# Branch products of a token mixer's merge as three fp32r products of split operands, with part of a later gate's work moved

## What is computed

```python
mod = silu(c) @ ada_w + ada_b            # 1024 -> 6 * 1024
shift1, scale1, gate1, shift2, scale2, gate2 = split(mod, 6)
...
ya = einsum('bsw,wd->bsd', o_att, w_branch_att)     # 512 -> 1024
yh = einsum('bsw,wd->bsd', o_hg, w_branch_hg)       # 512 -> 1024
g = sigmoid(gate_logits)                            # two gates of 1024
merged = g[:, :, 0] * ya + g[:, :, 1] * yh
x = x + gate1 * (merged @ w_out)
h = rms_norm(x, norm_ffn_w) * (1 + scale2) + shift2
x = x + gate2 * expert_choice_ffn(h, ...)
```

## Time and profile before

| what | us |
|---|---|
| runs of before, lowest / median / highest | 2107.93 / 2107.97 / 2111.01 |
| the profiled execution's own time | 2108.66 |
| its span | 2106.9 |
| branch products, first record | 393.07 |
| output product, first record | 499.2 |
| output product, last addition by DVE | 548.3 |
| first expert matmul | 594.75 |

### The profile page before, as it was taken

The page is one execution under the profiler, slowest core; times in us unless marked ns, Lnnn a source line. Parts: engine busy times, 40 slices in busy tenths (PEclk is TensorE's granted clock), DMA queues, the critical chain, the costliest instruction groups (busy, mean ns, idle before and its releaser), DMA issues.

```text
span 2106.9 us, 20424 instructions
## 1 busy us (share of the span) xinstructions
PE 1923.8 (91%) x8738; PEld 1153.0 (55%) x8738; DVE 670.3 (32%) x931; ACT 448.6 (21%) x673; POOL 28.7 (1%) x41
## 2 busy tenths in 40 slices
PE   5999989999689999898988998888899999999998
PEld 5876766567444343343434334342344588888887
DVE  5474474475411110202011010201129623222333
ACT  5357446212211000010100001010020313222222
POOL 0000000000000000000000000000030000000000
PEclk9999999999889999999999999999999999999999
DMA  7311210584669999999999999999951032332311
GB/s 296 97 44 41 63 38 21 202 283 174 259 253 416 417 418 418 417 416 417 416 416 417 418 418 417 417 416 416 380 163 60 20 100 85 96 100 100 100 60 40
DMA packets 149183, 513.42 MB, mean 244 GB/s; under 512 B 8035, under 2 KB 74723, under 8 KB 114147
## 3 DMA queue, kind: packets, MB, share of 16 engines
q1 hardware_dynamic: 144720, 487.95, 59.3%
q10 hardware_dynamic: 4374, 24.18, 3.0%
HBM read 510.00 MB, written 2.10 MB: 243 GB/s over the span
## 4 chain that ended last, share of the span: by engine, by line
PE 67%; DMA 21%; DVE 6%; ACT 4%; issue 2%; SPq 0%; POOL 0%; ACTq 0%; DVEq 0%; POOLq 0%
DMA work<-in_w_exp_up 13%; PE ps L1100 11%; PE ps L1061 6%; DMA ring<-in_w_exp_up 6%; PE ps L1263 5%; PE ps L521 5%; PE ps L1222 4%; PE ps L1223 4%; PE ps L1224 4%; PE ps L537 3%; PE ps L539 3%; PE ps L538 3%; PE ps L988 3%; PE ps L544 3%; PE ps L720 2%
## 5 line engine op out<-in xcount | busy, mean ns | idle before, releaser
L1061 PE MATMUL ps<-work 128*64 128x512 f32 x1208 | 331.4, 595 | 34.9 <-DMA work<-in_w_exp_up 34.9
L1061 PE MATMUL ps<-ring,work 128*64 128x512 f32 x720 | 218.8, 595 | 19.8 <-DMA ring<-in_w_exp_up 19.8
L1061 PEld LDWEIGHTS ps<-work 128*64 128x64 f32 x1208 | 112.0, 137 | 209.5 <-issue 142.3
L2167 DVE TENSOR_TENSOR work<-work,ps 64x512 f32<-64x512 f32 x64 | 42.0, 692 | 495.2 <-ACT work L1629 494.5
L1629 ACT ACTIVATE work<-ps 64x512 f32<-64x512 f32 x64 | 32.6, 584 | 751.1 <-PE ps L1061 751.1
L521 PE MATMUL ps<-work,ring 128*128 128x512 f32 x320 | 138.9, 592 | 0.7 <-issue 0.7
L1100 PE MATMUL ps<-work 128*64 128x512 f32 x568 | 135.4, 630 | 4.2 <-issue 3.6
L1061 PEld LDWEIGHTS ps<-ring,work 128*64 128x64 f32 x720 | 71.7, 137 | 122.8 <-issue 84.4
L1222 PE MATMUL ps<-xh,wh 128*128 128x512 f32 x352 | 137.0, 389 | 0.0
L1224 PE MATMUL ps<-xh,wl 128*128 128x512 f32 x352 | 136.9, 389 | 0.0
L1223 PE MATMUL ps<-xl,wh 128*128 128x512 f32 x352 | 136.9, 389 | 0.0
(11 more groups left out here) (311 smaller groups left out, 2531.7 us busy)
## 6 DMA issues: line engine op xcount, KB each, us to landing
work<-in_w_exp_gate SPq DMA_DIRECT2D x76, 1024.0 KB, 24.5
work<-in_w_exp_up SPq DMA_DIRECT2D x75, 1024.0 KB, 25.9
work<-in_w_exp_down SPq DMA_DIRECT2D x71, 1024.0 KB, 21.0
ring<-in_w_exp_gate SPq DMA_DIRECT2D x45, 1024.0 KB, 24.5
ring<-in_w_exp_up SPq DMA_DIRECT2D x45, 1024.0 KB, 25.5
ring<-in_w_exp_down SPq DMA_DIRECT2D x42, 1024.0 KB, 22.0
ring<-in_w_in SPq DMA_DIRECT2D x27, 1024.0 KB, 6.4
work<-in_ada_w ACTq DMA_DIRECT2D x16, 1024.0 KB, 6.1
```

The lines of the kernel that those rows point to most:

```text
L1061: i = e.matmul(PS[64 * gu:64 * gu + 64, fb, :], at(XET + 128 * k + 64 * z, 64), flat(key)[:, 512 * fb:512 * fb + 512], start=(k == 0), sto ...
```

## The change

The branch products go from `dense_T` to a new function `branch` with three fp32r products. Their operands are split in new places: the pieces `cb` by `cb_hi` (ACT) and `cb_lo` (DVE), the two branches' outputs by copies `OAH`, `OHH` (ACT) and subtractions `OAL`, `OHL` (DVE). For d = 0 the recurrence product comes first. The first gate's row and the second shift's columns go from d = 6 behind units 0 and 1 of the output product, and their evacuations with them. The first piece of `w_out` is loaded behind the last `cb` piece, into another slot; `x` is loaded in two halves, the first two chunks later. The cycle of the experts' slots and the conditions of their first use are adapted.

```diff
-    i = more.index(("c0", 3))
+    i = len(more)
-    slots.insert(len(slots) - len(more) + i, 16)
+    slots.insert(len(slots) - len(more) + i, 14)
-    cycle = (12, 13, 14, 15, 8, 16, 2, 4, 7, 11, 9, 10, 1, 5, 3, 0, 6)
+    cycle = (2, 13, 12, 16, 15, 8, 7, 11, 14, 4, 9, 10, 1, 5, 3, 0, 6)
...
                 if key == ("wo", 0):
-                    e.wait_ge(s["mg_m"], 1)
+                    e.wait_ge(s["mg_pb"], 6)
...
-                    if slot in (8, 2):
+                    if slot in (2, 13):
                         e.wait_ge(s["wo_pe"], 4)
+                    elif slot == 8:
+                        e.wait_ge(s["ac_pe"], 4)
+                        e.wait_ge(s["ar_pe"], 2)
                     elif slot in (9, 10, 1, 3):
                         e.wait_ge(s["wo_pe"], 8)
-                    elif slot in (12, 13, 14):
+                    elif slot in (12, 16):
                         e.wait_ge(s["mg_pb"], 8)
-                        e.wait_ge(s["mg_m"], 4)
```

On PE:

```diff
+            def branch(bk, half, j, off, hi, lo, each=None):
+                wl = FWL[plan["cb", half][0]]
+                for k in range(4):
...
+                    e.matmul(bank(bk), CBH[half][:, w], hi[:, x], start=(k == 0), stop=False)
+                    e.matmul(bank(bk), CBH[half][:, w], lo[:, x], start=False, stop=False)
+                    p = e.matmul(bank(bk), wl[:, w], hi[:, x], start=False, stop=(k == 3))
+                return p
...
                 if j == 0:
-                    e.wait_ge(*got[kb])
-                if d == 6:
-                    e.wait_ge(s["d_ada"], 16)
-                    e.wait_ge(s["mg_a"], 6)
-                    ada_row(ACC1, 0, 6)
-                    e.wait_ge(s["mg_b"], 6)
-                    ada_row(ACC1, 512, 7)
+                    e.wait_ge(s["fs_l"], (2, 4, 5, 6)[half])
                 if d == 0:
...
+                    e.wait_ge(s["sx_l"], 2)
+                    branch(b0 + 3, half, j, 4, OHH, OHL).then_inc(s["mg_pb"], 1)
+                    branch(b0 + 2, half, j, 0, OAH, OAL, lambda k: e.wait_ge(s["sx_l"], 3 + k)).then_inc(s["mg_pa"], 1)
+                    continue
...
-                dense_T(b0 + 2, kb, j, lambda k: at(OATT + 512 * k, 512), nk=4).then_inc(s["mg_pa"], 1)
+                branch(b0 + 2, half, j, 0, OAH, OAL).then_inc(s["mg_pa"], 1)
...
-                dense_T(b0 + 3, kb, j, lambda k: at(OHG + 512 * k, 512), nk=4, off=4).then_inc(s["mg_pb"], 1)
-                if d == 6:
-                    e.wait_ge(s["ar_a"], 1)
-                    ada_cols(ACC1, 1, 6, 0).then_inc(s["ac_pe"], 1)
+                branch(b0 + 3, half, j, 4, OHH, OHL).then_inc(s["mg_pb"], 1)
+
+            def second_gate(u):
+                if u == 0:
+                    e.wait_ge(s["d_ada"], 16)
+                    e.wait_ge(s["mg_a"], 8)
+                    ada_row(ACC1, 0, 6)
+                    e.wait_ge(s["mg_b"], 8)
+                    ada_row(ACC1, 512, 7)
+                elif u == 1:
+                    e.wait_ge(s["ar_a"], 1)
+                    ada_cols(ACC1, 1, 6, 0).then_inc(s["ac_pe"], 1)
...
                     ada_cols(ACC2, 0, 7, 0).then_inc(s["ac_pe"], 1)
```

On ACT (the two steps of `branch_hi` for piece 0 and the two for the recurrence output are woven behind the levels; piece 1 stands ahead of `ada_load(8)`):

```diff
                 def head_pair(pair):
+                    e.activation(OAH[:, 512 * pair:512 * pair + 512], bank(7), ACT.Copy)
                     e.activation(at(OATT + 512 * pair, 512), bank(7), ACT.Copy).then_inc(s["at_o"], 1)
...
-            e.dma_start(at(X, 4096).rearrange("p (c d) -> p c d", c=4), xv).then_inc(s["l_x"], 16)
+            e.dma_start(at(X + 2048, 2048).rearrange("p (c d) -> p c d", c=2), xv[:, 2:4, :]).then_inc(s["l_x"], 16)
+            for o in (0, 1024):
+                cb_hi(1, o, 1024)
...
             for d in range(4, 8):
                 i = d - 4
-                if d == 7:
-                    wo_hi(0)
                 e.wait_ge(s["mg_ga"], i + 1)
...
                 e.activation(at(mt[4 * (d % 2)], 512), bank(4 * (d % 2)), ACT.Tanh, scale=0.5).then_inc(s["mg_sa"], 1)
+                if d in (4, 6):
+                    cb_hi(d // 2, 0, 2048)
+                elif d == 7:
+                    wo_hi(0)
...
-                    ada_row(0, GATE1, 0.5)
...
-            for k in range(2, 8):
+            for k in range(2, 7):
                 merged_hi(k)
+            e.wait_ge(s["mg_pa"], 8)
+            e.dma_start(at(X, 2048).rearrange("p (c d) -> p c d", c=2), xv[:, 0:2, :]).then_inc(s["l_x"], 16)
+            merged_hi(7)
             wo_hi(2)
             wo_hi(3)
+            ada_row(0, GATE1, 0.5)
```

On DVE:

```diff
+            for pair in range(4):
+                x = slice(512 * pair, 512 * pair + 512)
+                e.wait_ge(s["at_o"], pair + 1)
+                e.tensor_tensor(OAL[:, x], at(OATT + 512 * pair, 512), OAH[:, x].bitcast(F32), ALU.subtract).then_inc(s["sx_l"], 1)
+            for i in range(2):
+                cb_lo(1, 1024 * i, 1024, i + 3)
...
                 else:
                     s0, s1 = mt[4 * (d % 2)], mt[4 * (d % 2) + 1]
                     two_ada(d)
+                    if d in (4, 6):
+                        cb_lo(d // 2, 0, 2048, d // 2 + 3)
```

More of the change, by code:

```diff
@@ L351, in rooms_of @@
             return piece(key, 4 if kind == "wo" else 8)
-        FS0, SX0 = 4, 8
+        FS_WO, FS0 = 6, 10
+        SXH_WO, SXH0 = 2, 10
+        SXL_WO, SX0 = 6, 14
         I2 = {3: 3, 1: 4, 2: 7, 0: 8, 5: 10, 4: 12}
@@ L1514, in _, with cb_hi, branch_hi @@
             weave(seq(hg_gate(0, (0, 1)), at_proj()), seq(hg_levels(0), hg_out(0)))
+            def cb_hi(half, o, n):
+                e.wait_ge(*got["cb", half])
+                if half < 2:
+                    e.wait_ge(s["lv_pe"], 52)
+                    e.wait_ge(s["lv_og"], 4)
+                else:
+                    e.wait_ge(s["mg_m"], 4 if half == 2 else 2)
+                e.activation(CBH[half][:, o:o + n], flat(("cb", half))[:, o:o + n], ACT.Copy).then_inc(s["fs_h"], 1)
+            def branch_hi():
+                for o in (0, 1024):
+                    cb_hi(0, o, 1024)
+                    yield
+                for o in (0, 1024):
+                    e.activation(OHH[:, o:o + 1024], at(OHG + o, 1024), ACT.Copy).then_inc(s["sx_h"], 1)
+                    yield
             att, hg = attention(), hg_proj(1)
             weave(hg, att, until=hg)
-            lv, gate, fill = seq(hg_levels(1), hg_out(1)), hg_gate(1, (2, 2)), branch_gates()
+            lv, gate, fill = seq(hg_levels(1), hg_out(1), branch_hi()), hg_gate(1, (2, 2)), branch_gates()
             weave(lv, gate, until=gate)
@@ L2005, in _, with cb_lo, branch_lo @@
             weave(seq(hg_gate(0, (0, 1)), at_proj()), seq(hg_levels(0), hg_out(0)))
+            def cb_lo(half, o, n, count):
+                e.wait_ge(s["fs_h"], count)
+                e.tensor_tensor(FWL[plan["cb", half][0]][:, o:o + n], flat(("cb", half))[:, o:o + n], CBH[half][:, o:o + n].bitcast(F32),
+                                ALU.subtract).then_inc(s["fs_l"], 1)
+            def branch_lo():
+                for i in range(2):
+                    cb_lo(0, 1024 * i, 1024, i + 1)
+                    yield
+                for i in range(2):
+                    x = slice(1024 * i, 1024 * i + 1024)
+                    e.wait_ge(s["sx_h"], i + 1)
+                    e.tensor_tensor(OHL[:, x], at(OHG + 1024 * i, 1024), OHH[:, x].bitcast(F32), ALU.subtract).then_inc(s["sx_l"], 1)
+                    yield
             att, hg = attention(), hg_proj(1)
             weave(hg, att, until=hg)
-            lv, gate, fill = seq(hg_levels(1), hg_out(1)), hg_gate(1, (2, 2)), branch_gates()
+            lv, gate, fill = seq(hg_levels(1), hg_out(1), branch_lo()), hg_gate(1, (2, 2)), branch_gates()
             weave(lv, gate, until=gate)
             weave(lv, fill, att, fill, att)
+            for pair in range(4):
+                x = slice(512 * pair, 512 * pair + 512)
+                e.wait_ge(s["at_o"], pair + 1)
+                e.tensor_tensor(OAL[:, x], at(OATT + 512 * pair, 512), OAH[:, x].bitcast(F32), ALU.subtract).then_inc(s["sx_l"], 1)
+            for i in range(2):
+                cb_lo(1, 1024 * i, 1024, i + 3)
             mt = [PT + 512 * i for i in range(8)]
```

73 lines of the change are left out of this document (39 added, 34 removed).

## The result

The changed kernel takes 2129.57 us, the median of four runs (2126.61 to 2130.44); the kernel before took 2108.34 beside it (2107.93 to 2111.01). The ratio is 1.0093, with an interval of 1.0081 to 1.0106: 21 us slower. The forecast was 2120 us, with a range from 2108 to 2127; the time lies 2.6 us beyond it. Direction and main cause were right; the size was 9.6 us short.

The account below looks back on a forecast made before the run. PE bounds the merge and output product, whose delay passes through the experts' stage to the end. Gain 10.8 us against losses of 22.7 gave net 11.9 (12.1 by stages) slower: 2120 us, range 2108 to 2127.

Parts of the forecast that it names:

- attention stage later by: Attention stage, ahead of the merge: split copies and subtractions on ACT and DVE cost 1.0 us, from nothing to 3 us.
- second gate product of d = 4 starts, after a wait of: Merge, first half: PE, ready at 421.7 us, waits for DVE's remainder until 428.0, so 6.3 us instead of 2.5.
- branch d = 6 starts, after a wait of: Merge, second half: PE waits 2.0 us (none to 5) for piece 3's remainder behind steps 20 and 21, until 485.1 us.
- four passes: Branch products: the skill's FP32 rule would save 1.7 us per d, 13.7 in all; the forecast used 1.35 and 10.8.
- the wait for `cb_lo(2)`: Branch products of d = 4: PE waits 12.7 us, from 435.4 to 448.1, for piece 2's remainder behind steps 16 and 17.
- The experts' weights: Ahead of the experts' stage: later loads end at about 583 us, 25 us before the first expert, costing zero.
- so little was shared, and I add nothing: Loads for d = 6: piece 3 and the `w_out` piece on SP's queue add nothing to ACT's loads of 2 MB.
- The sentence that I set aside: Loads for d = 6: engines take packets from queues in turn, which would put the forecast about 3 us higher.
- 3.4 us on PE as before: Output product: first gate's row (1.72 us) and second shift's columns (1.68 us), moved behind units 0 and 1, are not saved.
- More waits: Rival: attention costs 3 us, step 17's load or piece 3 come 2 to 4 us later; 2124 to 2127 us, chance 0.14.
- Faster: Rival in the merge: DVE's chain speeds up enough to hide `cb_lo(2)`; a gain of 4.7 us, 2103 us, chance 0.10.
- No change: Rival: DVE's idle time all goes, first load 2 us sooner, remainder at 443.3 us; 2110.5 us, chance 0.06.

Follow-up runs that it names:

- e1: The changed kernel with piece 2 copied behind step 15's load and subtracted between steps 14 and 15, not behind 16 and 17: 2115.22 us, ratio 1.0028 to before.
- e7: The changed kernel with loads of steps 20 and 21 issued behind ACT's high half of piece 3, its low half made earlier on DVE: 2127.09 us, 1.0080 to before.
- e2: The changed kernel with the first w_out piece's load issued only after the first gate product of d = 6: 2127.88 us, ratio 1.0088 to before.
- e3: The changed kernel with the second scale's columns behind unit 2 and its last row behind unit 3, one unit later each: 2126.50 us, ratio 1.0085 to before.
- e9: The changed kernel with DVE, ACT, SP and PE orders laid out anew, both gate products of d = 7 ahead of d = 6's branches: 2103.48 us, 0.9973 to before.
- e4: The changed kernel with the edits of e1, e2 and e3, and both first-gate halves and piece 3's remainder early: 2112.79 us, ratio 1.0018 to before.
- b1: The kernel before, its products unchanged, with only the halves of the first gate's row made earlier on ACT and DVE: 2110.24 us, ratio 1.0005 to before.
- e6: The changed kernel with the edits of e2 and e3 and DVE's program of the merge laid out anew: 2111.17 us, ratio 1.0007 to before.
- b2: The kernel before, keeping its fp32 products, with the order of e9 laid over it: 2115.18 us, ratio 1.0023 to before.
- e10: e9 with the low by low product added to each branch product, so four matmuls for three: 2108.88 us, ratio 0.9998 to before.

## Why the prediction was right and wrong, point by point

| step of the prediction | forecast | measured |
|---|---|---|
| attention stage later by | 1.0 | 0.9 (393.07 to 393.96; luck, see below) |
| three products of a d | 0.23 us apart | 0.23 to 0.24 |
| second gate product of d = 4 starts, after a wait of | 428.0, 6.3 | 430.24, 6.91 |
| branch d = 4 starts, after a wait of | 448.1, 12.7 | 449.95, 12.23 |
| branch d = 6 starts, after a wait of | 485.1, 2.0 | 489.20, 4.00 |
| d = 7 starts | 490.6 | 497.7 |
| wait in the output product | 1.3 | 1.4 |
| last unit done | 559.6 | 568.3 |
| first expert | 607 | 616.40 |

**Right.** The experts' stage keeps its length and passes everything on (1512.2 us in both). PE gets the matmul rate that the rows gave: PE reaches the second gate product of d = 4 at 423.3 us (430.24 less 6.91), 28.2 us of work behind the start without the 1.2 us bank wait, where 27.6 were forecast from the rows. By the Trainium skill's four passes (FP8 and Floating Point Precision, TensorE Precision Notes) the gain would be 1.7 us for each d; these rows, 6.87 us before and 5.5 now, have 1.35. The largest term, the wait for `cb_lo(2)` behind steps 16 and 17, was right in place, cause and size (both of its ends came about 2 us late), and e1 confirms it by taking it away. The experts' weights cost nothing, as forecast. That the attention stage took 0.9 us more where I had 1.0 is luck: the same program reaches the branch products at 391.7 us in e1 and 396.0 in e7, so one pair of traces can't tell 1 us from none.

**Wrong: the second half.** Up to branch d = 4 the forecast was 1.8 us short. The shorter `x` load did bring the first step sooner (404.09 us against 405.24 before), and ACT issued its load at 394.27 us, while the copies of piece 1 (394.08 and 395.04) ran and not behind them as I had it. But this was lost again at step 13. DVE's timeline of after, then of before:

```profile
426.58 2.35 DVE L1830 SCALAR_TENSOR_TENSOR work<-work,stay 128x2048 f32<-128x2048 f32 x1 [3.00 <-DMA work<-in_ada_w]
...
425.07 2.35 DVE L1782 SCALAR_TENSOR_TENSOR work<-work,stay 128x2048 f32<-128x2048 f32 x1 [0.61 <-DMA work<-in_ada_w]
```

The load of this step took 7.2 us, issued 0.9 us behind SP's piece 2; before it took 5.1, issued 1.4 us ahead of that piece. PE had got faster, so the piece was fetched sooner and fell on the load. That the one slowed the other is likely by what e7 shows for piece 3, but no run takes it apart. So the remainder came at 430.2 us instead of 428.0, and step 15 ended at 440.3 us, as before, where I had 438.4. Then three terms were missing or too small.

The first is "so little was shared, and I add nothing". I read from the trace of before that loads on SP's and ACT's queues hardly slow each other. In the change they are issued together: SP's piece 3 at 474.72 us, ACT's two loads of `ada_w` at 474.28. Piece 3 took 10.1 us; in e7, which moves ACT's loads behind it, it landed in 4.6. The sentence that I set aside, of the Trainium skill (DMA: Bandwidth & Descriptors, Queues, rings and completion order), says that engines take from the queues in turn, and e7 agrees with it. The rows I used had SP's piece issued 1.5 us behind ACT's loads; they showed what ACT's loads suffer, not what SP's piece does. Its own landing could be read in that trace too: 8.5 us. My 482.8 us had left 8.8 for it without saying so (482.8 less 472.1 and the copy's 1.92), so the step that failed, nothing for the sharing, is 1.3 us of the 2.0 by which this wait was too short.

The second is the clock. I charged 1.9 us behind the waits of 6.3 and 12.7 us and nothing behind the one in d = 6, since I had it at 2.0 us. It was 4.0, and the eight branch products behind it took 8.5 us (489.20 to 497.72) instead of 5.52: 3.0 us. A wait that is 2 us too long cost 5. That I had nothing behind a wait of 2.0 us was right by e1, where such a wait lost 0.1 us; what failed is that the range of the wait, up to 5 us, carried no clock with it. The size is in part chance: behind waits of 3.5 and 3.7 us in the same place, e2 and e3 lost 1.7.

The third is work moved together. I counted the columns that went behind unit 1 as "3.4 us on PE as before". But now the scale's stand right behind the shift's, 3.6 us without a wide matmul, and the clock fell to half behind them: 1.7 us by the window, 1.5 us of the stretch in e3.

By stages, the first expert was late against the forecast by 9.4 us: 1.8 ahead of branch d = 4, 0.3 in d = 4 and 5, 2.0 in the wait ahead of branch d = 6, 3.0 behind it, 1.6 in the output product (the columns), and 0.7 in the norm and router stage, which I can't place. "More waits" was the nearest rival and stopped at 2127, as it priced waits without the clock behind them: 3.0 us more would have reached the measured time.

**The rivals.** *Faster* had DVE's chain hide `cb_lo(2)`. It didn't, but the same place decides: e1 moves it and recovers 14.4 of 21.2 us. Its own price, a gain of 4.7 us with no wait left, is what e9 came near to by order (6.2). *No change* needed a chain 4.8 us faster; none was.

## What to carry to other kernels

When a product is split to save matmul time, its operands become work of the other engines, and a remainder that PE hangs on must stand ahead of everything on those engines that waits for a load. Price such a wait with the lower clock behind it (1.5 to 3.0 us each behind the waits of 2.5 us and more here), and read, for each load issued near it on another queue, what it does to the piece that is awaited. Then lay out the engines' programs for the whole stage at once, since moving one item can only move the wait (e4, b1, e6).

## What the runs showed of the hardware that I had not expected

- 32 one-column matmuls in a row, 3.6 us (columns of two parts behind one unit), brought PE's clock down although PE was busy without a break: 0.83 from 530 to 540 us. Set behind two different units, they left it at 1.00 (e3).
- In the merge the 24 matmuls behind a wait, 5.5 us at full clock, took 5.7 us behind waits of 0.5 and 2.0 us (e1) and 2.3 us (e6). In the kernels with all three products, and in the two with fp32 products, they took 7.0 to 8.5 us behind the waits of 2.5 to 12.9 us. The loss of 1.5 to 3.0 us did not grow with the wait: it was 3.0 behind 4.0 us and 2.2 behind 12.2 us in the same kernel. In b2's output product a wait of 2.3 us, 6.6 us behind the start of the matmuls after another wait, was followed by the lower clock too.
- The second half of a 1 MB piece took 10.1 us to land beside 2 MB issued at the same time on another queue, 8.5 in the kernel before, where they were issued 1.5 us ahead of the piece, and 4.6 without them (e7); 1 MB right behind it on its own queue made only 0.5 us of difference (e2).
- 14.7 us of matmuls added to a kernel with 5.0 us of waits cost 5.4 us, or 6.8 by the stretch (e10 against e9): filling waits also gives back the clock that they cost.
